# Three fused transformer blocks on one core: tanh in place of Silu in the neighbourhood phase, a rejoin by halves, later weight pieces in the second head, and other steps moved or halved

## The reference

```
x = first_block(x)    # gated linear attention, 4 heads, beside a chunked spatial gate; projection out
x = second_block(x)   # mLSTM in two directions, 4 heads, beside window attention; FFN with an embedding gate
x = third_block(x)    # gated DeltaNet in two directions beside neighbourhood attention; FFN
```

```
qkv = silu(short_conv(h_qkv, conv_w))              # 12 blocks of 128 channels, 5 taps
q, k = l2_normalize(q), l2_normalize(k)            # 8 of the 12
o    = rms_norm(o, norm_g) * silu(z)               # z: 4 blocks of 128 channels
o_na = neighborhood_attention(q_na, k_na, v_na, rpb)   # 8 heads of 64, softmax over a 2-D window
```

## Time and profile before

| | us |
|---|---|
| median of 3 runs | 4164.63 (4163.83 to 4167.79) |
| the profiled execution's own time | 4168.8 |
| its span in the trace | 4167.4 |
| PE busy in the span | 3869.9 (93%) |
| DVE, ACT, POOL busy | 1688.3, 1338.9, 387.1 |

### The profile page before, as it was taken

The page is one execution under the profiler, slowest core; times in us unless marked ns, Lnnn a source line. Parts: engine busy times, 40 slices in busy tenths (PEclk is TensorE's granted clock), DMA queues, the critical chain, the costliest instruction groups (busy, mean ns, idle before and its releaser), DMA issues. The chain is left out here.

```text
span 4167.4 us, 52748 instructions
## 1 busy us (share of the span) xinstructions
PE 3869.9 (93%) x21004; PEld 3051.1 (73%) x21004; DVE 1688.3 (41%) x2773; ACT 1338.9 (32%) x2310; POOL 387.1 (9%) x273
## 2 busy tenths in 40 slices
PE   9998999988998889999999999998688789999998
PEld 5776887866667668888888666666577668888886
DVE  3343323124565553222222444555456544333234
ACT  4354223123565241111111255555433232111112
POOL 1000000020005030000000320000233130000001
PEclk9999999989999999999999999999798899999999
DMA  2001011121103111111111121111200011111111
GB/s 89 28 28 56 26 48 48 45 80 34 36 31 92 41 41 51 45 51 45 49 47 47 40 69 34 53 48 51 82 32 32 32 36 46 48 48 50 46 50 56
DMA packets 85979, 199.40 MB, mean 48 GB/s; under 512 B 18712, under 2 KB 20184, under 8 KB 85800
## 3 DMA queue, kind: packets, MB, share of 16 engines
q1 hardware_dynamic: 85800, 196.96, 15.0%
HBM read 183.75 MB, written 15.14 MB: 48 GB/s over the span
## 5 line engine op out<-in xcount | busy, mean ns | idle before, releaser
L398 ACT ACTIVATE b_ffn_wh<-b_ffn_raw 128x1024 fp32r<-128x1024 f32 (+1 forms) x140 | 146.0, 1043 | 612.9 <-PE b_ffn_space L384 612.9
L383 PE MATMUL b_ffn_space<-b2f_x_lo,b_ffn_wh 128*128 128x512 f32 x800 | 316.0, 395 | 0.0
L382 PE MATMUL b_ffn_space<-b2f_x_hi,b_ffn_wh 128*128 128x512 f32 x800 | 314.1, 393 | 0.0
L384 PE MATMUL b_ffn_space<-b2f_x_hi,b_ffn_wl 128*128 128x512 f32 x800 | 312.0, 390 | 0.0
L450 DVE TENSOR_TENSOR b_ffn_wl<-b_ffn_raw,b_ffn_wh 128x1024 fp32r<-128x1024 f32 (+1 forms) x140 | 182.0, 1300 | 220.4 <-ACT b_ffn_wh L398 190.0
L382 PE MATMUL b_ffn_space<-b3f_hidden_hi,b_ffn_wh 128*128 128x512 f32 x512 | 199.2, 389 | 0.0
L383 PE MATMUL b_ffn_space<-b3f_hidden_lo,b_ffn_wh 128*128 128x512 f32 x512 | 199.2, 389 | 0.0
L384 PE MATMUL b_ffn_space<-b3f_hidden_hi,b_ffn_wl 128*128 128x512 f32 x512 | 199.2, 389 | 0.0
L383 PE MATMUL b_ffn_space<-b3f_x_lo,b_ffn_wh 128*128 128x512 f32 x480 | 189.3, 394 | 0.0
L382 PE MATMUL b_ffn_space<-b3f_x_hi,b_ffn_wh 128*128 128x512 f32 x480 | 187.3, 390 | 0.5 <-DVE b_ffn_wl L450 0.5
L384 PE MATMUL b_ffn_space<-b3f_x_hi,b_ffn_wl 128*128 128x512 f32 x480 | 186.9, 389 | 0.0
(11 more groups left out here) (621 smaller groups left out, 9002.4 us busy)
## 6 DMA issues: line engine op xcount, KB each, us to landing
b_ffn_raw<-w SPq DMA_DIRECT2D x64, 512.0 KB, 3.6
b_ffn_raw<-w_ffn SPq DMA_DIRECT2D x44, 512.0 KB, 3.6
all_x<-xT SPq DMA_DIRECT2D x16, 512.0 KB, 8.2
b_out_raw<-w_out SPq DMA_DIRECT2D x16, 512.0 KB, 3.7
b_ffn_raw<-w_ffo SPq DMA_DIRECT2D x16, 512.0 KB, 3.6
g_heads<-na_done SPq DMA_DIRECT2D x16, 512.0 KB, 2.9
na_feed_raw<-w_gqkv SPq DMA_DIRECT2D x24, 256.0 KB, 3.2
b_head_raw<-w_bv SPq DMA_DIRECT2D x16, 256.0 KB, 4.2
```

The lines of the kernel that those rows point to most:

```text
L382: nc.tensor.matmul(acc[i][:, c], wh[i][:, wk], xh[:, c], start=(k == 0), stop=False)
L383: nc.tensor.matmul(acc[i][:, c], wh[i][:, wk], xl[:, c], start=False, stop=False)
L384: last = nc.tensor.matmul(acc[i][:, c], wl[i][:, wk], xh[:, c], start=False, stop=(k == st.KT - 1))
L398: nc.scalar.activation(wh[i][:, 0:st.KT * P], raw[i][:, 0:st.KT * P], ACT.Copy).then_inc(hi_done, 1)
```

## The change

Seven edits, and due times that follow from them:

1. Neighbourhood phase, Silu. With h = x/2, silu(x) = h + h*tanh(h). The taps are halved once (`half_taps`), the take of a z block is a copy scaled by 0.5. For each half of each of the 16 blocks ACT writes tanh into the tile `gate`, POOL multiplies it by h and adds the product to h. There is one `gate` tile: the next tanh waits for POOL's addition (`gated`), and so do the norm's square and the store.
2. Neighbourhood phase, order. Transposes, `placing`, `gathering` and `gathered` are due 1.0 later, the norms' spread and scaling steps 1.2 later; a head's norm and store follow its new times.
3. Neighbourhood phase, rejoin. `joining` is all on DVE, by halves of 512 tokens: the first half of the 8 blocks is due before the last norm, then five blocks of the second half, and three more between the norm's steps.
4. Second head. `w_at` goes from 2.5 to 7.5, and the loads of the second half of x from -31 to 8.0 and on.
5. Linear attention. `turning_back` and `outputs` are due 1.5 later.
6. mLSTM. `finishing` makes two divisions and a sum of 128x1024 as four and two of 128x512.
7. `project_chain`. The first two weight blocks are loaded, rounded and subtracted in halves; PE still waits for the whole block.

```diff
@@ project_chain
-                        sp.dma_start(raw[i][:, 0:stages[0].KT * P], stages[0].w[i]).then_inc(w_landed[i], 16)
+                        sp.dma_start(raw[i][:, 0:cut], stages[0].w[i][:, 0:cut]).then_inc(first_landed[i], 16)
+                        sp.dma_start(raw[i][:, cut:2 * cut], stages[0].w[i][:, cut:2 * cut]).then_inc(w_landed[i], 16)
...
+                    if first:
+                        cut = st.KT * P // 2
+                        se.wait_ge(first_landed[i], 16)
+                        nc.scalar.activation(wh[i][:, 0:cut], raw[i][:, 0:cut], ACT.Copy).then_inc(first_hi, 1)
+                        se.wait_ge(w_landed[i], 16)
+                        nc.scalar.activation(wh[i][:, cut:2 * cut], raw[i][:, cut:2 * cut], ACT.Copy).then_inc(hi_done, 1)
+                        return
...
+                        ve.wait_ge(first_hi, i + 1)
+                        nc.vector.tensor_tensor(wl[i][:, 0:cut], raw[i][:, 0:cut], wh[i][:, 0:cut], ALU.subtract)
+                        cols = slice(cut, 2 * cut)
@@ LinearAttention.turning_back, outputs
-                yield self.unit_at(w) + 8.2 + 0.25 * b
+                yield self.unit_at(w) + 9.7 + 0.25 * b
...
-                yield self.unit_at(w) + 9.2 + 0.5 * b
+                yield self.unit_at(w) + 10.7 + 0.5 * b
@@ mlstm, finishing
+                            for t in (slice(0, DT // 2), slice(DT // 2, DT)):
+                                yield at + 9.0 + 1.5 * dr + 0.75 * (t.start // 4)
...
+                            yield at + 12.0 + 0.75 * (t.start // 4)
+                            ve.wait_ge(divided, 4 * h + 4)
+                            nc.vector.tensor_tensor(hsum[:, t], hsum[:, t], body[:, 1, t], ALU.add)
@@ second_block, norm_of
-                                yield -35.0 + 4 * h + i
+                                yield 8.0 + 2.0 * i if h else -35.0 + i
...
-                    return [norm], added, (13.2, 27.3), 1.75, 2.5, {"sync": [loads], "gpsimd": [], "scalar": [], "vector": [adding]}
+                    return [norm], added, (13.2, 27.3), 1.75, 7.5, {"sync": [loads], "gpsimd": [], "scalar": [], "vector": [adding]}
@@ HeadNorms
-                yield self.starts[m] + 6.5 + 2.0 * half
+                yield self.starts[m] + 7.7 + 2.0 * half
...
-                yield self.starts[m] + 7.5 + 2.0 * half
+                yield self.starts[m] + 8.7 + 2.0 * half
@@ neighbourhood_attention
+        gate, half_taps = ph.sb("gate", [P, HALF]), ph.sb("half_taps", [P, 12 * TAPS])
...
-                return nc.scalar.activation(done[m % 3][:, c], acc[:], ACT.Silu)
+                return nc.scalar.activation(done[m % 3][:, c], acc[:], ACT.Copy, scale=0.5)
...
-            return start + 1.85 * length + 1.0
+            return curve_time(m, 1) + 4.0
+
+        def curve_time(m, half):
+            start, length = plan[heads[m]]
+            if m > 12:
+                return start + length * (half + 1) / 2 + 0.3
+            return start + (1.8 if m < 12 else 1.0) * length + (0.2 if m < 12 else 2.6) + 3.5 * half
...
-                pool.wait_ge(feed.acc_ready[1], len(kinds))
-                join_blocks(nc.gpsimd, (pair, x), range(5, DT))
+                for m in range(len(heads)):
+                    for half in range(2):
+                        pool.wait_ge(curved, 2 * m + half + 1)
+                        h = done[m % 3][:, half * HALF:(half + 1) * HALF]
+                        nc.gpsimd.tensor_tensor(gate[:], gate[:], h, ALU.mult).then_inc(folded, 1)
+                        pool.wait_ge(folded, 2 * m + half + 1)
+                        nc.gpsimd.tensor_tensor(h, h, gate[:], ALU.add).then_inc(gated, 1)
...
-                            yield begin + w * SPACE + 7.0 + 2.0 * j
+                            yield begin + w * SPACE + 8.0 + 2.0 * j
...
-                        yield begin + w * SPACE + 12.0
+                        yield begin + w * SPACE + 13.0
...
-                    for k in range(5):
-                        yield plan[-1][0] + plan[-1][1] + 2.0 + 1.3 * k
-                        if k == 0:
-                            ve.wait_ge(feed.acc_ready[1], len(kinds))
-                        join_blocks(nc.vector, (pair, x), (k,))
+                    for half in range(2):
+                        c = slice(half * HALF, (half + 1) * HALF)
+                        for k in range(DT):
+                            yield norms.starts[-1] - 10.0 + 5.8 * half + 0.7 * k if half == 0 or k < 5 else norms.starts[-1] + 5.6 + 2.0 * (k - 5)
+                            if k == 0:
+                                ve.wait_ge(feed.acc_ready[half], len(kinds))
+                            nc.vector.tensor_tensor(x[:, k, c], pair.hi[:, k, c], pair.lo[:, k, c], ALU.add)
...
+                def curving():
+                    for m, i in enumerate(heads):
+                        for half in range(2):
+                            yield curve_time(m, half)
+                            if m < 12:
+                                se.wait_ge(conv.tapped, 2 * TAPS * m + 2 * TAPS - 1 + half)
+                            else:
+                                se.wait_ge(feed.taken[half], i + 1)
+                            if m or half:
+                                se.wait_ge(gated, 2 * m + half)
+                            nc.scalar.activation(gate[:], done[m % 3][:, half * HALF:(half + 1) * HALF], ACT.Tanh).then_inc(curved, 1)
```

More of the change, by code:

```diff
@@ L394, in high @@
                     st, b = stages[s], begin[s]
+                    if first:
[5 more added lines that the diff above has]
+                        return
                     se.wait_ge(w_landed[i], 8 * b + 16 * j + 16)
-                    if not first:
-                        se.wait_ge(acc_ready, b + 2 * j + i - 1)
+                    se.wait_ge(acc_ready, b + 2 * j + i - 1)
                     nc.scalar.activation(wh[i][:, 0:st.KT * P], raw[i][:, 0:st.KT * P], ACT.Copy).then_inc(hi_done, 1)
@@ L446, in _, with low @@
             def _(ve):
-                def low(s, j, i):
+                def low(s, j, i, first=False):
                     cols = slice(0, stages[s].KT * P)
+                    if first:
+                        cut = stages[s].KT * P // 2
+                        ve.wait_ge(first_hi, i + 1)
+                        nc.vector.tensor_tensor(wl[i][:, 0:cut], raw[i][:, 0:cut], wh[i][:, 0:cut], ALU.subtract)
+                        cols = slice(cut, 2 * cut)
                     ve.wait_ge(hi_done, begin[s] + 2 * j + i + 1)
@@ L476, in first_weights @@
                         yield lead.weights_at + i + 0.5
-                        low(0, 0, i)
+                        low(0, 0, i, True)
                 if lead is not None:
@@ L481, in _ @@
                 else:
-                    low(0, 0, 0)
-                    low(0, 0, 1)
+                    low(0, 0, 0, True)
+                    low(0, 0, 1, True)
                 split_low(nc, ve, split[2:], rounded, split_done, 2)
@@ L3704, in smoothed @@
         def smoothed(m):
-            return lambda se: se.wait_ge(conv.smoothed, m + 1)
+            return lambda se: se.wait_ge(gated, 2 * m + 2)
         def attended(b):
@@ L3751, in storing @@
                             n = norms.index(head_time(m))
-                            yield norms.starts[n] + 11.5
+                            yield norms.starts[n] + 12.7
                             sp.wait_ge(norms.scaled, 2 * n + 2)
@@ L3755, in storing @@
                             yield head_time(m)
-                            sp.wait_ge(conv.smoothed, m + 1)
+                            sp.wait_ge(gated, 2 * m + 2)
                         else:
-                            yield plan[i][0] + plan[i][1] + 0.1
-                            for half in range(2):
-                                sp.wait_ge(feed.taken[half], i + 1)
+                            yield curve_time(m, 1) + 4.0
+                            sp.wait_ge(gated, 2 * m + 2)
                         sp.dma_start(dram["g_heads"][m * P:(m + 1) * P, :], done[m % 3][:]).then_inc(stored[m % 3], 16)
@@ L3902, in gathered @@
                     for w, (b, pr) in enumerate(units):
-                        yield begin + w * SPACE + 14.0
+                        yield begin + w * SPACE + 15.0
                         se.wait_ge(o_ready, w + 1)
                         nc.scalar.activation(nq[:, b, pr * P:(pr + 1) * P], o[:, 0:P], ACT.Copy).then_inc(o_taken, 1)
-                weave(feed.high(se), feed.taking(se), conv.smoothing(se), exponentials(), placing(), gathered(), norms.squares(se), norms.roots(se))
+                def curving():
[9 more added lines that the diff above has]
+                            nc.scalar.activation(gate[:], done[m % 3][:, half * HALF:(half + 1) * HALF], ACT.Tanh).then_inc(curved, 1)
+                weave(feed.high(se), feed.taking(se), curving(), exponentials(), placing(), gathered(), norms.squares(se), norms.roots(se))
```

22 lines of the change are left out of this document (12 added, 10 removed).

## The result

The changed kernel takes 4124.35 us (median of 4, 4119.72 to 4133.82); beside it the kernel before took 4166.21. The ratio is 0.9897, 95% interval 0.9882 to 0.9911: 42 us faster, where 60.5 were forecast. 4124 lies inside the forecast's range, 4078 to 4134. On a second chip the two took 4127.35 and 4172.44 (ratio 0.9893, 0.9878 to 0.9908).

The account below looks back on a forecast made before the run. PE was taken as the bound, busy 3869.9 of 4167.4 us, so only its waits and clock could be won. Terms -12.5 - 30 - 7 - 5.5 - 3 - 2.5 = -60.5 from 4168.8, less 4.2, gave 4104 us; range 4078 to 4134.

Parts of the forecast that it names:

- rival 1: Neighbourhood: waits come back elsewhere, ACT behind POOL or transposes behind delayed scalings; units -12 instead of -30, 4122 to 4126; chance 0.20.
- Neighbourhood units: Neighbourhood phase: shorter PE waits -24, clock -9, POOL's cost +3, together -30 us; bounds -45 and -8.
- 10 for the move, 3 for the loads: Neighbourhood, 2480 to 2890: later transposes save 10 us of PE idle time, fewer table loads 3.
- I take back 9: Neighbourhood: lower clock loses 14.4 us; with most longer waits gone, 9 us of it come back.
- I charge 3; bounds 0 and 24: Neighbourhood: POOL's 64 gate passes delay DVE by 24 us of DVE time; 3 us charged, DVE being half idle.
- Rejoin: Neighbourhood's end: joins by halves free DVE earlier for the last norm's reciprocal; -7 us, bounds -4 and -7.4.
- Second head: Later weights and split x loads end ACT's 10.48 us wait, DVE's first scaling 14 us earlier; -12.5, bounds -6 and -14.
- rival 2: Second head: weights set the pace through SP's `w_low` waits; -6 instead of -12.5, 4111; chance 0.10.
- mLSTM: mLSTM: halved DVE passes shorten six of 14 `mlstm_state` waits by 0.6 us each; -3, bounds 0 and -5.
- Linear attention: Linear attention: moving back 1.5 plan units (1.05 us) shortens nine waits, 11.0 us; -5.5, at most 8.7, low bound -2.
- Tanh with a table of its own: Neighbourhood: tanh loads its own table, about 34 more loads than before; units +15 instead of -30, 4149; chance 0.05.
- Rival 4, the port: Neighbourhood: POOL passes falling on scalings before transposes each hold PE 1.25 us, 80 in all; about 4181; chance 0.03.

Follow-up runs that it names:

- the later kernel whose clock reads 1.00 there: Changed kernel with gate fold on DVE (very last half's behind eight half joins), mLSTM passes whole, four raw weight buffers in second head: 4107.85 us.
- Edit 2 alone: Kernel before with only the neighbourhood's later due times (transposes, placing, gathering, gathered, norm steps); Silu, table loads and rejoin as before: 4140.67 us.
- the fold on DVE: Changed kernel with POOL's two gate passes per half replaced by one DVE pass, POOL idle in the neighbourhood phase: 4118.96 us.
- Silu back on ACT: Changed kernel with the tanh form of Silu taken back; later due times and rejoin by halves kept: 4118.43 us.
- edit 2 alone taken back: Changed kernel with the neighbourhood's transposes, placing, gathering, gathered and norm steps at their old due times; tanh and rejoin kept: 4143.31 us.
- The kernel whose ACT waits for no weight piece: Changed kernel with four raw weight buffers instead of two in the second head, and mLSTM's divisions whole, sum still by halves: 4119.47 us.
- the idle-pass kernel: Changed kernel with the gate folded by DVE in one pass, plus 64 POOL passes of 64x512 on a spare tile nobody waits for: 4131.92 us.

## Why the prediction was right and wrong

**The whole.** The direction and most mechanisms held, the size did not: 42 us came of 60.5. That 4124 is also the time of rival 1 (4122 to 4126) is chance: rival 1 has 12 us from the neighbourhood's units, and they gave 24; the rest of the gap lies in other stages. And one of my signs of being wrong came true without being wrong: ACT waited for POOL 14.0 us in sum, more than 10.

**Neighbourhood units (-30; measured -24).** The sum was near, its terms were not. "10 for the move, 3 for the loads" and 11 for the late stretch made 24 of idle time, POOL took 3 of it back, and the clock made 9. In the changed kernel PE's idle time fell by 22.1, near the 21 of the sum. What is missing is the term "I take back 9": the granted clock over the stretch did rise, from 0.97 to 0.98, but PE's busy time fell by 1.8 us only. By "the clock loses 0.02 x 410 + 0.08 x 78 = 14.4 us" I had taken the lost share of the clock for lost time. Even in the later kernel whose clock reads 1.00 there, PE's busy time is only 8.2 us less than before.

The idle time came right by errors that cancel. Edit 2 alone gives 28.5: the waits for `na_wide` and `na_near` fell by 25 (39.9 to 14.7), PE's busy time by 3.2. I let each wait shrink by one k step, 0.7 us. Those for `na_near` did, by 0.6 on average (10.5 to 3.6 in 11 waits); those for `na_wide` fell by 1.5 (29.4 to 11.1 in 12). The two long ones went from 5.62 and 5.84 to 3.27 and 3.25. Around the first of these, in the kernel with edit 2 alone, PE has seven k steps instead of six between scores and wait, and ACT's copy of the product with v, for which it stood 1.31 us ahead of the exponentials, now comes behind the first two: the last exponential ends 9.98 us after the scores began, not 11.44. The move changed which steps meet, on ACT too; I had priced only the distance. Table loads, on top of the move and with the fold on DVE: 461.3 (Silu back on ACT) to 452.6, -8.7, where I had 3.

POOL: "I charge 3; bounds 0 and 24". It costs 12.0 us against the same fold on DVE, and this is the step that failed most in this phase: a cost put at 3 because "DVE is half idle". My 24 us of DVE time was right: scalings +13.0, taps +9.2, `wl` subtractions +2.2 (from the kernel with the fold on DVE to the changed one), 24.4. But I took the scalings for a quarter of it, by their count. They took over half, 13.0, and PE waits for them. The norm's 24 scalings, whose second operand lies in PSUM, kept their time: 690 ns at most in the `done` tiles and 749 in the q pairs, as before the change, though six of them overlap a POOL pass; taps reached 1778. The Trainium skill, SBUF — State Buffer, "Who interferes with whom", exempts a DVE instruction with at most one SBUF input outside the two-port modes; the trace agrees for the norm's scalings at 690 and 749 ns. It counts tensor_scalar among those that can enter such a mode; the 1498 ns of a scaling agree with that too.

**Rejoin (-7; measured -5.5 and -4.6).** The mechanism is right: 7.2 and 7.8 us in the two kernels where the joins went without a long stop, edit 2 alone taken back and Silu back on ACT. In the changed kernel the last scalings, the joins and the gate collide. POOL, in the first profile:

```profile
2941.39 5.74 POOL L3801 TENSOR_TENSOR na_gate<-na_gate,na_done 128x512 f32<-128x512 f32 x1 [3.49 <-ACT na_gate L3950]
```

DVE over the same stretch:

```profile
2936.27 1.92 DVE L3896 TENSOR_SCALAR na_near<-na_near,na_total 128x512 f32<-128x512 f32 x2
2938.11 7.90 DVE L3905 TENSOR_TENSOR all_x<-b3v_x_hi,b3v_x_lo 128x512 f32<-128x512 f32 x13
2945.93 0.93 DVE L3612 RECIPROCAL na_norm_rows<-na_norm_rows 16x128 f32<-16x128 f32 x1
2946.80 2.55 DVE L3905 TENSOR_TENSOR all_x<-b3v_x_hi,b3v_x_lo 128x512 f32<-128x512 f32 x2
```

The reciprocal starts 6.30 us after the last product's last matmul (2939.63), against 12.57 before (2968.19 and the earlier trace rows); then two joins, 1.21 us when alone, take 2.55 beside POOL, and PE's second spread waits for them. In the second profile of the same kernel the collision went the other way, POOL first:

```profile
2936.91 1.53 POOL L3801 TENSOR_TENSOR na_gate<-na_gate,na_done 128x512 f32<-128x512 f32 x1 [3.49 <-ACT na_gate L3950]
```
```profile
2933.63 10.04 DVE L3905 TENSOR_TENSOR all_x<-b3v_x_hi,b3v_x_lo 128x512 f32<-128x512 f32 x13
```

Here the 13 joins take 10.04 us instead of 7.90, the reciprocal comes 8.45 us after the last matmul, and the two joins behind it take their 1.21. The rejoin is left with 5.5 us in the first case and 4.6 in the second. The bound of -4, "POOL's gate slows the joins", had named this.

**Second head (-12.5; measured -7.7 and -7.3).** "Falls at about 910.6, 14 us earlier": 12 earlier. "That costs 1 to 2 us": from its first scaling to its last lowering DVE took 37.3 us instead of 34.0, and from there to the next stage PE took another 1.1 more. Of DVE's 3.3 us, 1.1 are the longer wait for the second root (2.73 against 1.67) and 1.8 two waits for PE's gate products (3.4 in the second profile, where DVE took 38.9 us). The kernel whose ACT waits for no weight piece has the wait for the second root too, so this part is not rival 2. What I left out is that the second half's root hangs on POOL's last pair, behind two lowerings that come early now; why the gate products come late is open. The step that failed is "paced by DVE (two passes per block), which nothing shortens": DVE also waits, for roots and for the gate products.

**mLSTM (-3; measured +4.6).** The wrong sign. "Six of the 14 waits stand behind one", so shorter passes would shorten them; I priced the passes alone and did not ask where the weave would put the state steps between more of them, nor what POOL does at that time. The bounds 0 and -5 excluded a loss without a reason.

**Linear attention (-5.5; measured -8.1 to -8.7)**, under-sized: PE's idle time fell by 6.3 us and its busy time by 2.4. `gla_on` waits fell from 11.0 to 3.9 us. The same code as before took 250.6 us in another profile, 2.0 more, so the last 2 us are not sure. **First weights (-2.5):** the waits fell by 2.3 in the first trace and by 1.9 to 3.6 over all kernels with halves, against the mean of 23.5 with whole blocks. The waits are as forecast; that the program got shorter by them isn't shown, since the stages around them vary by about as much among kernels with the same code. **Leads, 0:** nothing to see.

**Rivals.** Tanh with a table of its own: excluded by 23 loads. Waits that come back elsewhere: 5.7 us as `na_et`, and 8.9 and 5.1 as ACT's waits for POOL, of which the idle-pass kernel leaves no cost to see. Rival 4, the port, had the right mechanism at too high a price: 12 us lost, not 64. The gap of 18 us to the forecast is mLSTM 7.6, second head 5, units 6 and rejoin 2, less 3 from linear attention.

## What to carry to other kernels

Where the passes of two engines stop each other, give work to the idle one only if its passes meet nothing on the path: here one pass more on the busy engine was 12 us cheaper in the feed stretch than two on the idle one (9 us with the end counted, 15 once the last fold stood behind the joins). Splitting a pass into halves helps only if a waiting step really comes between them; look up where the queue puts it, and leave a loss inside the bounds. Moving steps back in an in-order queue was the largest single gain, 28.5 us; price it by what each step meets on every engine, not by the distance moved.

## What the runs showed of the hardware that was not expected

Which of DVE and POOL goes first where their passes collide is not fixed by the program. Beside the same run of DVE joins, in the same code, one POOL pass that takes 1.3 us alone took 5.74 in the changed kernel's first profile, while seven joins passed it at 0.68 each; in its second profile it took 1.53, and two joins took 1.75 each. Two further kernels with this code there show the first outcome (5.74), one the second (1.53).

What a DVE pass loses goes by the POOL pass and not by its own length. Beside POOL passes of 128x512 (1.3 us alone) a scaling of 484 ns took up to 1498, a tap of 747 up to 1778 and a `wl` subtraction of 692 up to 1793: 1.0 to 1.1 us each. Beside the idle passes of 64x512 (1.04 us) the scaling took up to 1262, 0.8 more. In the kernel before, beside POOL passes of 128x1024, a join of 1211 ns took 3353.

PE's busy time on the same products, over the neighbourhood's stretch, was 443.7 us at a granted clock of 0.97, 441.9 at 0.98, 437.3 at 0.99 and 435.5 at 1.00 (the kernel before, the changed one, the fold on DVE, and the later kernel with everything the runs point to).
